# One layer of a gated trunk: who makes the low parts of the weights in the up stage

## The chip, the cores and the metric

The kernel runs on one core of a Trainium2 chip. The metric is the device time of one execution in microseconds (us). TensorE does the matrix products, VectorE (DVE in the rows), ScalarE (ACT) and GpSimd (POOL) do elementwise work, and SyncE (SP), ScalarE and GpSimd issue transfers between the memory (HBM) and the on-chip SBUF. Rows with a q (ACTq, SPq) are an engine's instructions that issue transfers. PSUM is where TensorE writes, in eight banks of 512 columns.

## What is computed

One layer with batch 1, 512 tokens and width 1024: windowed attention and retention, then the PEER mixer, which takes the experts from two tables of 16384 rows, then a gated embedding and norms. The part that matters here, cut:

```python
h = rms_norm(x, mix_norm);  z = h @ w_in          # attention and retention mixers, gates
x = x + merged @ w_out
# peer(h = rms_norm(x, ffn_norm)): 8 heads, each picks 16 of 128*128 experts per token
q = (h @ w_query).reshape(B, S, PEER_HEADS, 2, half)
s1, s2 = q[..., 0, :] . sk[0],  q[..., 1, :] . sk[1]
top_s, expert_idx = top 16 of v1 + v2;  gates = softmax(top_s)
u  = jnp.take(expert_down, idx, axis=0)
act = jax.nn.gelu(jnp.einsum('td,ted->te', hx, u))
vv = jnp.take(expert_up, idx, axis=0)
y  = jnp.einsum('te,ted->td', act * g, vv)
x = x + y
gate = sigmoid(rms_norm(x, ple_norm) @ w_ple_gate);  x = x + gate * (p @ w_ple_proj)
return rms_norm(x, final_norm)
```

The kernel computes `act` for all 16384 experts and all tokens but the last 128 as dense products, in 128 units of 128 experts, with the gates of the experts not chosen at zero; the last 128 tokens go over fetched rows.

## The kernel before

**Numbers in two parts.** A product in fp32 is made of three products in fp32r: each operand is split into a high part (ScalarE's copy to fp32r) and a low part, the operand less the high part. `mm3` (lines 931 to 934) adds high x high, high x low and low x high in one bank.

**Weights.** All weights go through one ring of eight slots of 128x1024 (512 KB each), unit after unit in the order of `UNITS`: projections, then 128 units `dn` (the down table), 128 units `up` (the up table), two `pp`, eight `pg`. `UP0` is the number of the first up unit. For each unit SyncE reads the slot `raw` (line 480) once TensorE is done with the unit eight back (`wait_used`), ScalarE makes `w_hi` (line 550, `upper`, signal `hi_done`), and GpSimd makes `w_lo` as `raw - w_hi` (line 493, `lower`, signal `lo_done`). `raw` and `w_lo` lie at the same address, so `w_lo` is written in place. ScalarE runs `LEAD` = 5 units ahead in the two stages with the expert tables.

**Down stage.** For each unit `dn`, TensorE multiplies with h for the first 352 tokens (`down`), ScalarE applies gelu (line 754) and stores the activations in HBM. Beside it the gates are spread and stored, and GpSimd fetches rows of the down table for the remaining tokens (line 517), which VectorE multiplies and sums (line 1335, `dot`).

**Up stage.** For unit e, VectorE (`weigh`) multiplies activations and gates, read back by ScalarE in groups of four units (`read_back`, lines 790 and 793), to `wgt` (line 1754); ScalarE copies it to `b_hi` (line 846, `weight_upper`, two units ahead); VectorE makes `b_lo` (line 1763, signal `wgt_split`). Between the two, from unit 8 on, VectorE adds a fetched row of the up table times its activation into PSUM (`axpy`, lines 1740 and 1743), 128 rows in all, 15 in 16 units on the average, mostly one to a unit. TensorE (`up`) waits for `lo_done` and `wgt_split` of the unit and runs 18 matmuls of 512 columns: three tiles of tokens, two banks each, `mm3`. Six banks collect all 128 units.

**GpSimd's queue.** GpSimd goes through the units in one written order: wait for `hi_done` of unit u, make `w_lo`, then issue the fetches that stand at u. The fetches of the up table (line 529) stand from u = `UP0` + 5 on (`FETCH_UP`), each waits for its slot among ten (`V_SLOTS`): the first needs the gates stored and the embeddings split (`p_split`), the seventh all dots, the eleventh and later the `axpy` ten before it.

**ScalarE's order in the up stage** (`up_turn`), for unit e: `w_hi` of unit e + 5, then `b_hi` of unit e + 2, and at the end of each group of four a read-back.

Of the kernel before, what the change touches and what calls it, by code (L numbers as in the profile page):

```python
# [7 lines left out]
F32 = mybir.dt.float32  # L8
F32R = mybir.dt.float32r
U32 = mybir.dt.uint32  # L10
ALU = mybir.AluOpType
# [7 lines left out]
PH, NKEY, TOPK = 8, 128, 16  # L19
# [16 lines left out]
RING = 8  # L36
# [35 lines left out]
DN0, UP0 = UNIT[("dn", 0)], UNIT[("up", 0)]  # L72
# [66 lines left out]
FIRST_Z = 7  # L139
EXP_AT, SELECT_AT = 4, 6  # L140
AHEAD = 2
FINAL_DVE = 6
RAW_Q = 4

# [51 lines left out]
def block_program(nc, xT_d, w_d, small_d, rope_r_d, decay_d, rope_a_d, mask_d, pT_d, down_d, up_d, out_d):  # L196
# [14 lines left out]
    with ExitStack() as ctx:  # L211
# [3 lines left out]
        def sem(name):  # L215
            return ctx.enter_context(nc.semaphore(name))
# [3 lines left out]
        w_hi = sb("w_hi", [P, RING, UW], F32R)  # L220
        with nc.sbuf_tensor("raw", [P, RING, UW], F32) as raw:
            pass
        w_lo = sb("w_lo", [P, RING, UW], F32R)
# [128 lines left out]
        landed = [sem(f"landed{i}") for i in range(RING)]  # L352
        hi_done = sem("hi_done")
        lo_done = sem("lo_done")
        proj_done = sem("proj_done")
        proj_free, pg_free = [sem("proj_free0"), sem("proj_free1")], sem("pg_free")
        tile_ready, tile_free = sem("tile_ready"), sem("tile_free")
# [132 lines left out]
        @block.gpsimd  # L490
        def _(pool):
            def lower(s):
                return nc.gpsimd.tensor_tensor(w_lo[:, s, :], raw[:, s, :], w_hi[:, s, :].bitcast(F32),  # L493
                                               ALU.subtract)

            first = min(FETCH_DOWN) // RING
            with pool.Fori(0, first) as r:
                for s in range(RING):
                    pool.wait_ge(hi_done, RING * r + (s + 1))
                    lower(s).then_inc(lo_done, 1)  # L500
            for u in range(first * RING, NU):
                pool.wait_ge(hi_done, u + 1)
                lower(u % RING).then_inc(lo_done, 1)
                for r in FETCH_DOWN.get(u, ()):
                    extra, n = row_of(r)
                    if r == 0:
                        pool.wait_ge(x_spilled, 16)
                        pool.wait_ge(sq_ready, 2 * KT)
                        pool.wait_ge(h_ready, 3 * KT)
                    if extra:  # L510
                        pool.wait_ge(extra_ready, 1)
                    elif n % TOPK == 0:
                        pool.wait_ge(expert_ready, n // TOPK + 1)
                    if r >= U_SLOTS:
                        pool.wait_ge(dot_done, r - U_SLOTS + 1)
                    ids = expert_extra if extra else expert_of
                    pool.indirect_dma_start(u_slot(r), None, down_d,
                                            bass.IndirectOffsetOnAxis(ap=ids[:, n:n + 1], axis=0)
                                            ).then_inc(u_landed[r % U_SLOTS], 16)
                for n in FETCH_UP.get(u, ()):  # L520
                    if n == 0:
                        for b in range(2):
                            pool.wait_ge(gate_written[b], 16 * (NTG // 2))
                        pool.wait_ge(p_split, 2)
                    if n == V_OWN:
                        pool.wait_ge(dot_done, NROWS)
                    if n >= V_SLOTS:
                        pool.wait_ge(axpy_done, n - V_SLOTS + 1)
                    pool.indirect_dma_start(v_slot(n), None, up_d,
                                            bass.IndirectOffsetOnAxis(ap=expert_of[:, n:n + 1], axis=0)  # L530
                                            ).then_inc(v_landed[n % V_SLOTS], 16)
            for k in range(FINAL_DVE, KT):
                pool.wait_ge(x_ready, KT + k + 1 + (k == KT - 1))
                nc.gpsimd.tensor_scalar(final[:, k, :], xT[:, k, :], gains[:, 3, k:k + 1], None, ALU.mult
                                        ).then_inc(pool_scaled, 1)
            pool.wait_ge(pool_scaled, KT - FINAL_DVE)
            pool.wait_ge(rows_spread, 1)
            for k in range(FINAL_DVE, KT):
                nc.gpsimd.tensor_tensor(final[:, k, :], final[:, k, :], rrms, ALU.mult).then_inc(final_pool, 1)
# [3 lines left out]
        def _(sc):  # L543
# [304 lines left out]
            def up_turn(i):  # L848
                last = i == NKEY // STEP - 1
                for c in range(STEP):  # L850
                    e = STEP * i + c
                    upper(UP0 + LEAD + e, (UP0 + LEAD + e) % RING)
                    if not last or c + AHEAD < STEP:
                        weight_upper(e + AHEAD, (c + AHEAD) % STEP)
# [74 lines left out]
        def _(pe):  # L929
# [16 lines left out]
            def columns(key, r_hi, r_lo, kt=KT, u=None, at=0, width=P, tiles=None, at_tile={}):  # L946


                u = UNIT[key] if u is None else u
                pe.wait_ge(lo_done, u + 1)  # L950
                bank_free(key)
                s = u % RING
                for k in range(kt):
                    if tiles is not None:
                        pe.wait_ge(tiles[0], tiles[1] + k + 1)
                    if k in at_tile:
                        at_tile[k]()
                    o = k * width + at
                    ins = mm3(proj_bank(key), w_hi[:, s, o:o + P], w_lo[:, s, o:o + P],
                              r_hi[:, k, :], r_lo[:, k, :], k == 0, k == kt - 1)  # L960
                ins.then_inc(proj_done, 1)
# [263 lines left out]

            def up(i, c):
                e = STEP * i + c
                pe.wait_ge(lo_done, e + (UP0 + 1))
                pe.wait_ge(wgt_split, e + 1)
                first = isinstance(i, int) and i == 0 and c == 0  # L1230
                last = isinstance(i, int) and i > 0 and c == STEP - 1
                s = (UP0 + c) % RING
                for t in range(TDT):
                    a = slice(P * t, P * t + P)
                    for n, b in enumerate(UP_BANKS[t]):
                        if first and b == 0:
                            pe.wait_ge(act_ready, NKEY)
                        ins = mm3(bank[:, b, :], b_hi[:, c % 4, a], b_lo[:, c % 4, a],
                                  w_hi[:, s, 512 * n:512 * n + 512], w_lo[:, s, 512 * n:512 * n + 512], first, last)
                    if last and t < TDT - 1:  # L1240
                        ins.then_inc(up_tile_done, 1)
                ins.then_inc(up_done, 1)
# [40 lines left out]
                if m == 1:  # L1283
                    spread(2)
            last = UNIT[("pg", KT - 1)]
            pe.wait_ge(lo_done, last + 1)
            for x in range(2):
                pe.wait_ge(pg_free, KT - 4 + x)
                for k in range(KT):
# [13 lines left out]
        def _(ve):  # L1303
# [17 lines left out]
            tt, ts, stt = nc.vector.tensor_tensor, nc.vector.tensor_scalar, nc.vector.scalar_tensor_tensor  # L1321
# [424 lines left out]
            def weigh(e):  # L1746
# [13 lines left out]
                for n in ADD_UP_AT.get(e, ()):  # L1760
# [2 lines left out]
                tt(b_lo[:, c % 4, 0:TD], wgt[:, c % 2, :], b_hi[:, c % 4, 0:TD].bitcast(F32),  # L1763
                   ALU.subtract).then_inc(wgt_split, 1)

            for e in range(NKEY):
                weigh(e)

            def evict(t, b, at):

# [129 lines left out]
```

## Time and profile before

| | us |
|---|---|
| median of 3 runs | 1982.0 |
| lowest and highest | 1981.55, 1982.93 |
| span of the profiled execution | 1979.5 |
| TensorE busy in it | 1956.9 |
| VectorE, GpSimd, ScalarE busy | 1365.3, 1234.5, 806.0 |

The span runs from the first to the last instruction of one profiled execution; the runs are timed without a profile and include what lies around the span. The up stage lies between 1381 and 1904 us of the span. Engines overlap, so a busy time says nothing of the end by itself: what counts is whether TensorE waits.

### The profile page before, as it was taken

To read this page: it belongs to the slowest core of one execution; us is meant where nothing else is said; L and a number is where in the kernel's file an instruction comes from. 1 tells how busy PE (TensorE), PEld (TensorE's weight loads), DVE (VectorE), ACT (ScalarE), POOL (GpSimd) and SP (SyncE) were. 2 spreads that over 40 slices of the span, in tenths; PEclk is the share of its full clock that TensorE was granted. 3 is DMA by queue.
4 is the path that set the end of the run, shared out by engine and by line. 5 is a ranking of instruction groups with operands and counts; after the bars stand their busy time and mean duration, and the time that the engine had idled before them with its cause. 6 is when DMAs were issued, how large, how long until landed. Compare 5 with 4: busy or idle time off the path is not lost.

```text
span 1979.5 us, 27319 instructions
## 1 busy us (share of the span) xinstructions
PE 1956.9 (99%) x10232; PEld 1724.9 (87%) x10232; DVE 1365.3 (69%) x2287; ACT 806.0 (41%) x1272; POOL 1234.5 (62%) x686
## 2 busy tenths in 40 slices
PE   7999999999999999999999999999999999999998
PEld 6888888888888888999999999999888888888887
DVE  6433333332831489999968888861998999999976
ACT  5222222232553343433346666654333333333352
POOL 5343434352234433899997767766998988888842
PEclk9999999999999999999999999999999999999999
DMA  5222222233223332899997999998999999999931
GB/s 198 86 90 86 91 85 85 87 116 112 80 75 96 96 128 78 333 333 350 366 360 270 386 377 359 372 389 273 363 372 347 377 357 354 375 364 361 358 108 43
DMA packets 171953, 471.93 MB, mean 238 GB/s; under 512 B 13776, under 2 KB 62928, under 8 KB 170064
## 3 DMA queue, kind: packets, MB, share of 16 engines
q1 hardware_dynamic: 58032, 209.04, 30.5%
q0 software_dynamic: 41472, 151.01, 20.5%
q10 hardware_dynamic: 72352, 110.64, 15.6%
q8 instruction: 54, 0.88, 0.2%
q14 instruction: 43, 0.35, 0.0%
HBM read 413.49 MB, written 54.53 MB: 236 GB/s over the span
## 4 chain that ended last, share of the span: by engine, by line
PE 96%; DVE 2%; ACT 1%; DMA 0%; issue 0%; POOL 0%; POOLq 0%; SPq 0%; DVEq 0%; ACTq 0%
PE bank L932 29%; PE bank L934 29%; PE bank L933 29%; PE bank L1185 4%; PE bank L1047 1%; PE bank L1130 1%; PE bank L1115 1%; PE bank L1091 0%; PE bank L1101 0%; DVE bank L1375 0%; DMA xT<-x_cols 0%; PE bank L1016 0%; PE bank L1138 0%; ACT b_hi L594 0%; DVE h_lo L1383 0%; DVE scr L1422 0%
## 5 line engine op out<-in xcount | busy, mean ns | idle before, releaser
L493 POOL TENSOR_TENSOR w_lo<-raw,w_hi 128x1024 fp32r<-128x1024 f32 x390 | 937.3, 2412 | 650.1 <-ACT w_hi L550 646.9
L932 PE MATMUL bank<-h_hi,w_hi 128*128 128x352 f32 (+2 forms) x1560 | 549.1, 352 | 0.0
L934 PE MATMUL bank<-h_hi,w_lo 128*128 128x352 f32 (+2 forms) x1560 | 538.1, 345 | 0.0
L933 PE MATMUL bank<-h_lo,w_hi 128*128 128x352 f32 (+2 forms) x1560 | 537.2, 344 | 0.0
L550 ACT ACTIVATE w_hi<-raw 128x1024 fp32r<-128x1024 f32 x390 | 407.6, 1054 | 309.8 <-DMA raw<-weights 254.0
L933 PEld LDWEIGHTS bank<-h_lo,w_hi 128*128 128x128 f32 x1560 | 294.7, 189 | 19.7
L934 PEld LDWEIGHTS bank<-h_hi,w_lo 128*128 128x128 f32 x1560 | 293.0, 188 | 20.7
L932 PEld LDWEIGHTS bank<-h_hi,w_hi 128*128 128x128 f32 x1560 | 293.8, 188 | 19.5
L1763 DVE TENSOR_TENSOR b_lo<-scr,b_hi 128x384 fp32r<-128x384 f32 x128 | 267.3, 2088 | 46.3 <-ACT b_hi L846 46.1
L932 PE MATMUL bank<-w_hi,b_hi 128*128 128x512 f32 x768 | 298.9, 389 | 0.0
L934 PE MATMUL bank<-w_hi,b_lo 128*128 128x512 f32 x768 | 298.8, 389 | 0.0
L933 PE MATMUL bank<-w_lo,b_hi 128*128 128x512 f32 x768 | 298.8, 389 | 0.0
L932 PEld LDWEIGHTS bank<-w_hi,b_hi 128*128 128x128 f32 x768 | 144.2, 188 | 30.2 <-DVE b_lo L1763 0.5
L933 PEld LDWEIGHTS bank<-w_lo,b_hi 128*128 128x128 f32 x768 | 144.2, 188 | 30.0
L934 PEld LDWEIGHTS bank<-w_hi,b_lo 128*128 128x128 f32 x768 | 144.2, 188 | 29.8
L754 ACT ACTIVATE scr<-bank 128x352 f32<-128x352 f32 x128 | 58.7, 458 | 150.0 <-PE bank L934 149.9
L932 PE MATMUL bank<-b_hi,w_hi 128*128 128x512 f32 x272 | 108.2, 398 | 10.6 <-DVE b_lo L1350 9.2
L846 ACT ACTIVATE b_hi<-scr 128x384 fp32r<-128x384 f32 x128 | 66.7, 521 | 122.9 <-DVE scr L1754 122.5
L932 PE MATMUL bank<-w_hi,h_hi 128*128 128x512 f32 (+1 forms) x288 | 109.7, 381 | 1.1 <-DVE h_lo L1383 1.1
L934 PE MATMUL bank<-w_hi,h_lo 128*128 128x512 f32 (+1 forms) x288 | 108.8, 378 | 0.0
L933 PE MATMUL bank<-w_lo,h_hi 128*128 128x512 f32 (+1 forms) x288 | 108.7, 378 | 0.0
L1335 DVE SCALAR_TENSOR_TENSOR more<-more,bank 128x1024 f32<-128x1024 f32 x80 | 96.9, 1211 | 15.8 <-DMA more<-peer_down,scr 9.1
(227 smaller groups left out, 2705.0 us busy)
## 6 DMA issues: line engine op xcount, KB each, us to landing
raw<-weights SPq DMA_DIRECT2D x390, 512.0 KB, 6.2
act_scratch<-scr ACTq DMA_DIRECT2D x64, 384.0 KB, 7.1
gate_scratch<-scr ACTq DMA_DIRECT2D x12, 2048.0 KB, 13.5
scr<-gate_scratch ACTq DMA_DIRECT2D x22, 768.0 KB, 9.6
scr<-act_scratch ACTq DMA_DIRECT2D x22, 768.0 KB, 14.8
xT<-gate_scratch ACTq DMA_DIRECT2D x10, 768.0 KB, 8.9
xT<-act_scratch ACTq DMA_DIRECT2D x10, 768.0 KB, 14.9
scr<-scr ACTq DMA_DIRECT2D x20, 128.0 KB, 3.9
```

What stands on the lines that cost most here:

```text
L493: return nc.gpsimd.tensor_tensor(w_lo[:, s, :], raw[:, s, :], w_hi[:, s, :].bitcast(F32), ALU.subtract)
L550: nc.scalar.activation(w_hi[:, u_mod, :], raw[:, u_mod, :], ACT.Copy).then_inc(hi_done, 1)
L754: nc.scalar.activation(act[:, c % 4, 0:TZ], bank[:, c % 2, 0:TZ], ACT.Gelu_apprx_tanh).then_inc(act_ready, 1)
L846: nc.scalar.activation(b_hi[:, c % 4, 0:TD], wgt[:, c % 2, :], ACT.Copy).then_inc(wgt_hi_ready, 1)
L932: nc.tensor.matmul(out, a_hi, c_hi, start=first, stop=False)
L933: nc.tensor.matmul(out, a_hi, c_lo, start=False, stop=False)
L934: return nc.tensor.matmul(out, a_lo, c_hi, start=False, stop=last)
L1047: ins = nc.tensor.matmul(bank[:, 2 + j, 0:S - P * j], r_k[:, c, P * j:P * j + P], r_q[:, c, P * j:S], start=c == 0, stop=c == 1)
L1115: ins = nc.tensor.matmul(bank[:, 7, P * t:P * t + P], a_v[:, t - 1 + b, P * kv:P * kv + P], a_pT[:, t, b, :], start=b == 0 or t == 0, stop ...
L1185: ins = nc.tensor.matmul(scattered(q)[:, x, :], onehot(q, x, 0).bitcast(F32), gated[q % 4][:, x, :], start=True, stop=True)
L1335: stt(out=row, in0=row, scalar=1.0, in1=h_tok, op0=ALU.mult, op1=ALU.mult, accum_out=to[:, n:n + 1]).then_inc(dot_done, 1)
L1763: tt(b_lo[:, c % 4, 0:TD], wgt[:, c % 2, :], b_hi[:, c % 4, 0:TD].bitcast(F32), ALU.subtract).then_inc(wgt_split, 1)
```

## The change

In the up stage GpSimd makes `w_lo` of the first two units only (`OWN_LOW` = 2). VectorE makes the other 126 (`VE_LOW`), by `lower_up(e + 2)` behind `weigh(e)`, under a signal of its own, `up_lo_done`. TensorE's waits are renumbered. GpSimd keeps its row fetches in their written order, and the `w_lo` of all units before and after.

```diff
--- before.py
+++ after.py
@@ -139,6 +139,8 @@
 FIRST_Z = 7
 EXP_AT, SELECT_AT = 4, 6
 AHEAD = 2
+OWN_LOW = 2
+VE_LOW = NKEY - OWN_LOW
 FINAL_DVE = 6
 RAW_Q = 4
 
@@ -352,6 +354,7 @@
         landed = [sem(f"landed{i}") for i in range(RING)]
         hi_done = sem("hi_done")
         lo_done = sem("lo_done")
+        up_lo_done = sem("up_lo_done")
         proj_done = sem("proj_done")
         proj_free, pg_free = [sem("proj_free0"), sem("proj_free1")], sem("pg_free")
         tile_ready, tile_free = sem("tile_ready"), sem("tile_free")
@@ -499,8 +502,9 @@
                     pool.wait_ge(hi_done, RING * r + (s + 1))
                     lower(s).then_inc(lo_done, 1)
             for u in range(first * RING, NU):
-                pool.wait_ge(hi_done, u + 1)
-                lower(u % RING).then_inc(lo_done, 1)
+                if not UP0 + OWN_LOW <= u < UP0 + NKEY:
+                    pool.wait_ge(hi_done, u + 1)
+                    lower(u % RING).then_inc(lo_done, 1)
                 for r in FETCH_DOWN.get(u, ()):
                     extra, n = row_of(r)
                     if r == 0:
@@ -947,7 +951,7 @@
 
 
                 u = UNIT[key] if u is None else u
-                pe.wait_ge(lo_done, u + 1)
+                pe.wait_ge(lo_done, u + 1 if u < UP0 else u + 1 - VE_LOW)
                 bank_free(key)
                 s = u % RING
                 for k in range(kt):
@@ -1225,7 +1229,10 @@
 
             def up(i, c):
                 e = STEP * i + c
-                pe.wait_ge(lo_done, e + (UP0 + 1))
+                if isinstance(i, int) and e < OWN_LOW:
+                    pe.wait_ge(lo_done, e + (UP0 + 1))
+                else:
+                    pe.wait_ge(up_lo_done, e - (OWN_LOW - 1))
                 pe.wait_ge(wgt_split, e + 1)
                 first = isinstance(i, int) and i == 0 and c == 0
                 last = isinstance(i, int) and i > 0 and c == STEP - 1
@@ -1283,7 +1290,7 @@
                 if m == 1:
                     spread(2)
             last = UNIT[("pg", KT - 1)]
-            pe.wait_ge(lo_done, last + 1)
+            pe.wait_ge(lo_done, last + 1 - VE_LOW)
             for x in range(2):
                 pe.wait_ge(pg_free, KT - 4 + x)
                 for k in range(KT):
@@ -1763,8 +1770,16 @@
                 tt(b_lo[:, c % 4, 0:TD], wgt[:, c % 2, :], b_hi[:, c % 4, 0:TD].bitcast(F32),
                    ALU.subtract).then_inc(wgt_split, 1)
 
+            def lower_up(e):
+
+                s = (UP0 + e) % RING
+                ve.wait_ge(hi_done, UP0 + e + 1)
+                tt(w_lo[:, s, :], raw[:, s, :], w_hi[:, s, :].bitcast(F32), ALU.subtract).then_inc(up_lo_done, 1)
+
             for e in range(NKEY):
                 weigh(e)
+                if e + OWN_LOW < NKEY:
+                    lower_up(e + OWN_LOW)
 
             def evict(t, b, at):
 
```

On **VectorE**, at the start of the up stage (`scr` is the place of the activations and gates and of `wgt`), before and then after:

```order
L1754 TENSOR_TENSOR scr<-scr 128x384 [waits acts_landed0,gate_landed0]
L1763 TENSOR_TENSOR b_lo<-scr,b_hi 128x384 [waits wgt_hi_ready]
L1754 TENSOR_TENSOR scr<-scr 128x384
L1763 TENSOR_TENSOR b_lo<-scr,b_hi 128x384 [waits wgt_hi_ready]
L1754 TENSOR_TENSOR scr<-scr 128x384 [waits wgt_split]
L1763 TENSOR_TENSOR b_lo<-scr,b_hi 128x384 [waits wgt_hi_ready]
```

```order
L1761 TENSOR_TENSOR scr<-scr 128x384 [waits acts_landed0,gate_landed0]
L1770 TENSOR_TENSOR b_lo<-scr,b_hi 128x384 [waits wgt_hi_ready]
L1777 TENSOR_TENSOR w_lo<-raw,w_hi 128x1024 [waits hi_done]
L1761 TENSOR_TENSOR scr<-scr 128x384
L1770 TENSOR_TENSOR b_lo<-scr,b_hi 128x384 [waits wgt_hi_ready]
L1777 TENSOR_TENSOR w_lo<-raw,w_hi 128x1024 [waits hi_done]
L1761 TENSOR_TENSOR scr<-scr 128x384 [waits wgt_split]
L1770 TENSOR_TENSOR b_lo<-scr,b_hi 128x384 [waits wgt_hi_ready]
L1777 TENSOR_TENSOR w_lo<-raw,w_hi 128x1024 [waits hi_done]
```

A `w_lo` of 1024 columns now stands between the `b_lo` of one unit and the product of the next.

On **GpSimd**, at the seam of the down and the up stage (the seventeen `w_lo` ahead of the first fetch are those of the last eleven down units and the first six up units; x17 means seventeen alike in a row), before and then after:

```order
L493 TENSOR_TENSOR w_lo<-raw,w_hi 128x1024 [waits hi_done] x17
L529 DMA scr<-peer_up,scr 128x1024 [waits p_split,gate_written1,gate_written0]
L529 DMA scr<-peer_up,scr 128x1024
L493 TENSOR_TENSOR w_lo<-raw,w_hi 128x1024 [waits hi_done]
L529 DMA scr<-peer_up,scr 128x1024
L493 TENSOR_TENSOR w_lo<-raw,w_hi 128x1024 [waits hi_done]
```

```order
L496 TENSOR_TENSOR w_lo<-raw,w_hi 128x1024 [waits hi_done] x13
L533 DMA scr<-peer_up,scr 128x1024 [waits p_split,gate_written1,gate_written0]
L533 DMA scr<-peer_up,scr 128x1024 x5
L533 DMA more<-peer_up,scr 128x1024 [waits dot_done]
L533 DMA more<-peer_up,scr 128x1024 x3
L533 DMA scr<-peer_up,scr 128x1024 [waits axpy_done] x6
```

The first ten fetches now follow each other behind the `w_lo` of the second up unit, with no wait for a weight between them; the eleventh is the first that waits for a row addition (`axpy_done`).

## Rows read from the trace of the kernel before

**Rows 1.** The page: busy us of each engine (share of the span), instructions.

```profile
PE 1956.9 (99%) x10232; PEld 1724.9 (87%) x10232; DVE 1365.3 (69%) x2287; ACT 806.0 (41%) x1272; POOL 1234.5 (62%) x686
```

**Rows 2.** Windows: length, busy us of PE, PEld, DVE, ACT, POOL, clock, DMA share, GB/s.

```profile
1340.00:1381.00 41.00, 41.00 (x258) 41.00 (x257) 4.80 (x7) 17.68 (x25) 26.29 (x11) 1.00 0.85 272
...
1512.00:1643.00 131.00, 130.97 (x579) 108.14 (x578) 123.74 (x99) 48.83 (x65) 115.86 (x68) 1.00 1.01 366
...
1773.00:1904.00 131.00, 131.00 (x580) 108.51 (x579) 117.58 (x96) 49.16 (x65) 106.44 (x59) 1.00 0.90 324
```

**Rows 3.** TensorE in order of time: start us, us, engine, line, output<-inputs.

```profile
1381.49 0.39 PE L932 MATMUL bank<-w_hi,b_hi 128*128 128x512 f32 x1
...
1505.29 0.39 PE L932 MATMUL bank<-w_hi,b_hi 128*128 128x512 f32 x1
1505.51 0.39 PE L933 MATMUL bank<-w_lo,b_hi 128*128 128x512 f32 x1
...
1903.87 1.25 PEld L1255 LDWEIGHTS bank<-small,scr 128*128 128x128 f32 x10
```

**Rows 4.** The waits of TensorE in the stage, then what stands behind the one.

```profile
PEld bank L932 <- DVE b_lo L1763: 0.5, 1, 0.5
...
1510.14 6.25 ACTq L793 DMA_DIRECT2D scr<-act_scratch  x1
...
1517.94 2.45 DVE L1763 TENSOR_TENSOR b_lo<-scr,b_hi 128x384 fp32r<-128x384 f32 x1 [2.18 <-ACT b_hi L846]
```

**Rows 5.** Groups of the stage: busy us, mean ns | idle before, releaser.

```profile
L493 POOL TENSOR_TENSOR w_lo<-raw,w_hi 128x1024 fp32r<-128x1024 f32 x129 | 311.3, 2415 | 52.1 <-ACT w_hi L550 50.2
...
L1763 DVE TENSOR_TENSOR b_lo<-scr,b_hi 128x384 fp32r<-128x384 f32 x127 | 266.8, 2100 | 34.3 <-ACT b_hi L846 34.2
```

**Rows 6.** GpSimd and VectorE side by side, in order of time.

```profile
1500.45 2.39 POOL L493 TENSOR_TENSOR w_lo<-raw,w_hi 128x1024 fp32r<-128x1024 f32 x1
...
1501.19 2.08 DVE L1763 TENSOR_TENSOR b_lo<-scr,b_hi 128x384 fp32r<-128x384 f32 x1
...
1503.00 1.10 POOL L529 DMA_INDIRECT scr<-peer_up,scr  x1 [0.16 <-issue]
...
1503.19 0.55 DVE L1754 TENSOR_TENSOR scr<-xT 128x384 f32<-128x384 f32 x1
```

**Rows 7.** VectorE in order of time, where the feeders catch up.

```profile
1701.91 0.55 DVE L1754 TENSOR_TENSOR scr<-xT 128x384 f32<-128x384 f32 x1
1702.38 1.27 DVE L1743 SCALAR_TENSOR_TENSOR bank<-more,scr,bank 128x1024 f32<-128x1024 f32 x1
1703.57 2.09 DVE L1763 TENSOR_TENSOR b_lo<-scr,b_hi 128x384 fp32r<-128x384 f32 x1
1705.58 0.55 DVE L1754 TENSOR_TENSOR scr<-xT 128x384 f32<-128x384 f32 x1
```

**Rows 8.** The seam of down and up stage, GpSimd, ScalarE and VectorE, by time.

```profile
1370.48 4.77 POOL L493 TENSOR_TENSOR w_lo<-raw,w_hi 128x1024 fp32r<-128x1024 f32 x2 [4.10 <-ACT w_hi L550]
...
1374.91 1.06 ACT L550 ACTIVATE w_hi<-raw 128x1024 fp32r<-128x1024 f32 x1 [0.43 <-ACT scr L754]
...
1378.77 0.56 DVE L1763 TENSOR_TENSOR b_lo<-scr,b_hi 128x384 fp32r<-128x384 f32 x1 [11.96 <-ACT b_hi L846]
...
1381.70 0.46 ACT L754 ACTIVATE scr<-bank 128x352 f32<-128x352 f32 x1 [0.39 <-PE bank L934]
...
1383.13 1.46 ACTq L793 DMA_DIRECT2D xT<-act_scratch  x1
...
1386.14 2.45 DVE L1763 TENSOR_TENSOR b_lo<-scr,b_hi 128x384 fp32r<-128x384 f32 x1 [4.73 <-ACT b_hi L846]
...
1388.32 1.09 POOL L529 DMA_INDIRECT scr<-peer_up,scr  x1
```

**Rows 9.** Groups of VectorE by form, over the whole span.

```profile
L1690 DVE TENSOR_TENSOR b_lo<-bank,scr 128x1024 fp32r<-128x1024 f32 x48 | 58.7, 1222 | 14.4 <-PE bank L1185 14.3
```

**Rows 10.** The weight reads of line 480 issued in the up stage.

```profile
DMA to landing us min/median/max: 3.3/7.2/10.1
```


## The prediction

> **What bounds the kernel now.** I read the page first, then the windows of the up stage, then TensorE's rows at its two ends, then what VectorE and GpSimd do in one unit of it. The page gives TensorE 1956.9 us of the 1979.5 us span [rows 1]. The windows of the up stage, four of 130 to 131 us from 1381 to 1904 us of which the second and the fourth stand in the rows, show TensorE busy in all but 0.03 us, at the full granted clock, with the DMA engines marked busy nearly all the time and 324 to 366 GB/s moved [rows 2]. So in the stage that the change touches nothing but TensorE's own stream sets the pace.
>
> That stream can be measured at its ends. The first up matmul starts at 1381.49 us, and the transposes behind the last one are loaded at 1903.87 us [rows 3]: 522.38 us for 128 units of 18 matmuls, 226.7 ns each, **4.08 us a unit**. Two rows in the middle have the same step, 1505.29 to 1505.51 [rows 3]. TensorE waits once in the whole stage, 0.5 us, for a low part of the weighted activations [rows 4]. That is all that a change of the feeders can give back here.
>
> Who feeds it: per unit GpSimd makes w_lo, 2415 ns in the mean [rows 5], and issues a row fetch, 1.10 us [rows 6]. VectorE multiplies activations and gates (L1754), adds a fetched row (L1743) and makes b_lo (L1763). Where the feeders catch up, VectorE starts a unit at 1701.91 and the next at 1705.58 us [rows 7], a step of 3.67 us, just over the 2.41 + 1.10 of GpSimd, so it runs at GpSimd's pace. Two rows show why: b_lo takes 0.56 us at 1378.77 [rows 8] but 2100 ns in the mean [rows 5]. The one at 1501.19 us ends at 1503.27, 0.43 us after the end (1502.84) of the w_lo that GpSimd started at 1500.45 [rows 6]. The two operations exclude each other. This costs slack and no time, as 3.67 is below 4.08.
>
> **What is taken away.** 126 of the 129 w_lo of the stage leave GpSimd, 304 of their 311.3 us [rows 5]. With them the exclusion goes: b_lo, 266.8 us now [rows 5], should take 0.56 us each, some 71 us. On the path to the end this is worth the one wait, **-0.5 us**. Its history: ScalarE was held for 6.25 us, from 1510.14, in issuing a read of activations; b_hi was so late that b_lo started only at 1517.94, took 2.45 us, and ended at 1520.39 us [rows 4]. With 0.56 in place of 2.45 it would have been ready 1.9 us earlier, more than the 0.5 that were missing. I take the whole 0.5.
>
> **What is added.** 126 operations of 128x1024 on VectorE with two sources in SBUF. None of that size and those sources stands in the trace. Bounds: not under the one of 384 columns, 0.56 us [rows 8], and not over GpSimd's own 2.41 us for the same tile [rows 5]. The nearest row is VectorE's 1024-column operation with one source in PSUM, 1222 ns [rows 9], and I take that. An operation starts some 0.08 us before the one ahead has ended: L1754 to L1743 is 0.47 us, L1743 to L1763 is 1.19 [rows 7]. VectorE's unit is then 0.47 + 1.19 + 0.48 + 1.14 = 3.28 us, and 3.36 with the second row addition of every fifteenth unit. TensorE's is 4.08, so **VectorE stays faster by 0.72 us a unit** (now by 0.41), and the added work costs nothing. TensorE's stream hides it; that cover is gone only if w_lo takes more than 1.14 + 0.72 = 1.86 us up to the next start. By the Trainium skill ("VectorE: DVE Perf Modes", the part on mode 2x_2P) an fp32 tensor_tensor stays at one element a cycle, since both read ports are taken; 0.96 GHz makes an estimate of 1.07 us plus a fixed part, and the sum would not change.
>
> **The waits that are added.** lower_up(e+2) stands behind b_lo(e) and waits for w_hi of unit e+2. ScalarE makes that one a turn before b_hi(e), for which b_lo(e) has just waited, so in the loop the wait is always met. At the seam w_hi(3) starts at 1374.91 us and w_hi(2) before it, both ahead of VectorE's first b_lo at 1378.77 [rows 8]: met too. TensorE's wait for w_lo is met two units ahead, and b_lo stays what comes last. Queued behind the new operation is the product of the next unit, and behind that b_hi and b_lo. At the seam w_lo(2) delays the second product by 1.14 us, and with it ScalarE. There the last down activation, at 1381.70, had waited 0.39 us for TensorE [rows 8], so it moves by 0.75 and ends at 1382.9; TensorE wants it (for the bank of its third tile) 12 matmuls after 1381.49, at 1384.2. The read issue of 1383.13 moves to 1383.9 and lasts 1.46, and b_lo(2) starts 1.55 us after it as now [rows 8] and ends at 1387.5 us, for a unit due at 1381.49 + 2 x 4.08 = 1389.65. Now it ends at 1386.14 + 2.45 = 1388.59 [rows 8], the thinnest margin of the seam. Cost: nothing.
>
> **What moves without being written.** In GpSimd's queue the fetches for unit u stood behind the w_lo of unit u and so behind its w_hi. Now nothing paces them but free slots. The ten slots are free when GpSimd leaves w_lo(1), the first of the two that start at 1370.48 [rows 8], at about 1372.9 us. So ten fetches of 512 KB go out by about 1385, where now the first leaves at 1388.32 us [rows 8]. The stretch that they move into carries 272 GB/s [rows 2], and after it the queue is quiet until the first row addition. In the loop a fetch then leaves when a slot comes free, one each 4.3 us as now, and the bytes are the same in all. Beside the burst weights must still land: those of unit u are asked for when unit u-8 is done, and have 4 units less 2.4 us (w_hi, b_hi, b_lo and hand-offs), **13.9 us**, until b_lo(u-3) is late. Now they land in 7.2 us in the stage's median and 10.1 at most [rows 10]. Cost taken: nothing; its bounds are the first rival.
>
> The up loop on TensorE also loses seven register instructions; its rows have no gap where they stand, so nothing comes of it. The pp and pg weights stay on GpSimd, and what follows 1904 us is untouched.
>
> **Sum**: 0 (added) - 0.5 (the wait) + 0 (burst) = -0.5 us on the span of 1979.5. The three runs have a median of 1982.0, 2.5 us over the span, and I carry that over: **1981.5 us**. A measurement of this kernel can tell about 0.2%, 4 us, so this is "no change".
>
> **Rivals.**
>
> *The burst holds the weights (slower).* If the weight reads had to queue behind the ten fetches, 5.24 MB at 366 GB/s [rows 2] are 14.3 us, and a weight tile would land after 7.2 + 14.3 = 21.5 us, 7.6 over the allowed 13.9, once: **1989 us**. It decides from a landing time of 13.9 us. A milder form goes by ScalarE: the read issue at 1383.9 held for 6.25 us as at 1510.14 [rows 4] puts the end of b_lo(2) at 1392.2, 2.6 us late: 1984. For: the DMA engines are marked full in the stage [rows 2]. Against: weights land in 7.2 us now with a fetch in flight nearly always. Chance 6% for over 4 us, and 8% for the mild form, which counts as same.
>
> *Fetch issues hold VectorE (slower).* If the issue of a fetch excluded VectorE's two-source operations as w_lo does, its 1.10 us [rows 6] would come on top of VectorE's 3.36: 4.46 us a unit, 0.38 over TensorE's, times 120 units, +46 us: **2027 us**. It decides from 0.72 us held per unit. The trace speaks against it: the product at 1503.19 takes 0.55 us inside the fetch of 1503.00 to 1504.10, and the b_lo of 1501.19 ends 0.27 us into that fetch [rows 6]. Chance 2%. The Trainium skill ("SBUF — State Buffer", on the shared port pair) says that a VectorE operation with two SBUF inputs and a GpSimd operation that reads SBUF exclude each other for the whole instruction, and a fetch takes its row numbers from SBUF; these two rows don't bear that out for it.
>
> *VectorE is as slow at w_lo as GpSimd (slower).* At 2.41 us its unit is 3.36 - 1.14 + 2.33 = 4.55 us, 0.47 over, times 126: +59 us, **2040 us**. The row of 1222 ns is against it. Chance 1%.
>
> *The change doesn't do what it says*: should b_lo stay long or the wait come back elsewhere, the time is **1982**, within same. *TensorE is freed (faster)*: for over 4 us of gain its step of 226.7 ns would have to shrink by 1.7 ns, but the mean over the stage, in which w_lo alone keeps GpSimd busy for 311 us [rows 5], equals the step at 1505.29 [rows 3], when the fetch of 1503.00 has ended and no w_lo runs. Chance 2%.
>
> **How the numbers follow.** The forecast with its near forms (up to 3 us lost, or the wait kept) has 89%, of it 8% for the mild loss; burst 6%, ports 2%, slow w_lo 1%, faster 2%. So same 0.89, slower 0.09, faster 0.02. The range takes the runs' own spread (1981.55 to 1982.93) about 1981.5, the mild loss above and a microsecond below: 1980.3 to 1984.8.
>
> **What the profile after would show.** Right: TensorE's up stage 522 us long and without a wait; w_lo on VectorE near 1.22 us; b_lo near 0.56 us throughout; ScalarE waiting less for VectorE and more for weights; GpSimd's busy time down by some 300 us and VectorE's by 266.8 - 71 - 154 = 42; ten fetches from 1373 to 1385 us; weight landings under 13.9 us. Wrong: waits of TensorE for b_lo in units 2 to 8 (burst), w_lo or b_lo lengthened beside fetches (ports), or a VectorE that never rests in the stage (slow w_lo).

## The result, and the profile after

| | before | after |
|---|---|---|
| median of the runs, us | 1982.4 (4 runs) | 1992.1 (4 runs) |
| lowest and highest, us | 1981.55, 1982.93 | 1990.08, 1992.70 |
| span of the profiled execution, us | 1979.5 | 1990.9 |

The ratio is 1.005, with a 95% interval of 1.0037 to 1.0062: slower by some 10 us, where no change was forecast.

The page of the changed kernel, engines as in [rows 1]:

```profile
PE 1957.9 (98%) x10232; PEld 1724.6 (87%) x10232; DVE 1308.0 (66%) x2413; ACT 803.7 (40%) x1272; POOL 975.7 (49%) x560
```

GpSimd has lost 259 us and VectorE 57, as the edit meant. TensorE is busy 1 us longer, and the span is 11.4 us longer: TensorE waits somewhere. The windows of the up stage, columns as in [rows 2], say where:

```profile
1381.00:1512.00 131.00, 122.38 (x532) 100.61 (x531) 96.37 (x120) 47.44 (x64) 43.45 (x30) 0.97 0.95 344
1512.00:1643.00 131.00, 131.00 (x580) 108.47 (x579) 108.90 (x131) 48.29 (x64) 49.12 (x35) 1.00 0.99 363
1643.00:1773.00 130.00, 130.00 (x575) 107.67 (x574) 108.67 (x130) 47.74 (x64) 44.76 (x34) 1.00 0.99 362
1773.00:1904.00 131.00, 131.00 (x580) 108.47 (x579) 108.71 (x126) 47.12 (x63) 45.35 (x27) 1.00 0.90 326
```

The last three windows are full. All of the loss lies in the first, and all of TensorE's waits of the stage are these two (the waits, from 1384 us on: us in total, times, longest):

```profile
PE bank L936 <- DVE b_lo L1770: 7.3, 1, 7.3
PE bank L936 <- issue: 1.3, 1, 1.3
```

The first and the last of the ten fetches, then ScalarE, VectorE and TensorE, each in order of time; this is the seam of [rows 8]:

```profile
1373.28 0.95 POOL L533 DMA_INDIRECT scr<-peer_up,scr  x1
...
1386.85 0.94 POOL L533 DMA_INDIRECT more<-peer_up,scr  x1 [1.14 <-issue]
...
1385.61 0.46 ACT L758 ACTIVATE scr<-bank 128x352 f32<-128x352 f32 x1 [2.77 <-remote]
1386.53 0.43 ACTq L794 DMA_DIRECT2D xT<-gate_scratch  x1
1387.05 9.88 ACTq L797 DMA_DIRECT2D xT<-act_scratch  x1
1396.98 1.06 ACT L554 ACTIVATE w_hi<-raw 128x1024 fp32r<-128x1024 f32 x1 [10.16 <-issue]
1397.94 0.51 ACT L850 ACTIVATE b_hi<-scr 128x384 fp32r<-128x384 f32 x1
...
1398.48 0.56 DVE L1770 TENSOR_TENSOR b_lo<-scr,b_hi 128x384 fp32r<-128x384 f32 x1 [14.40 <-ACT b_hi L850]
...
1386.12 0.50 PE L936 MATMUL bank<-w_hi,b_hi 128*128 128x512 f32 x1 [1.32 <-issue]
...
1391.49 0.39 PE L938 MATMUL bank<-w_hi,b_lo 128*128 128x512 f32 x1
1399.18 0.77 PE L936 MATMUL bank<-w_hi,b_hi 128*128 128x512 f32 x1 [7.30 <-DVE b_lo L1770]
1399.75 0.63 PE L937 MATMUL bank<-w_lo,b_hi 128*128 128x512 f32 x1
1400.18 0.63 PE L938 MATMUL bank<-w_hi,b_lo 128*128 128x512 f32 x1
...
1403.59 0.40 PE L937 MATMUL bank<-w_lo,b_hi 128*128 128x512 f32 x1
```

Read it upwards. TensorE stops behind unit 1 and goes on at 1399.18, when b_lo(2) has ended (1398.48 + 0.56). b_lo(2) waited for b_hi(2), started at 1397.94. ScalarE came to it late because the instruction ahead, the issue of the third read-back's activations, lasted 9.88 us, where the same row took 1.46 in [rows 8]. While it lasted, the data of the ten fetches were still being moved. The share of the 16 DMA engines' time by queue while the issue was held, 1387 to 1397 us of the changed kernel (packets, MB, share):

```profile
q0 software_dynamic: 608, 2.22, 55.2%
q1 hardware_dynamic: 364, 1.36, 34.1%
q10 hardware_dynamic: 345, 0.50, 13.4%
```

q0 is GpSimd's queue, q1 SyncE's (the weights), q10 ScalarE's. ScalarE's queue moved 0.50 MB in these 10 us. In the kernel before, in the ten microseconds from the same issue (1383 to 1393 us), it moves 1.97 MB in 58.1% of the engines' time, and q0 only 0.45 MB.

**Where the 11.4 us go.** TensorE's next matmul was due at 1391.72 (0.23 us a step) and came at 1399.18: 7.46. The ten matmuls from there start 0.43 to 0.57 us apart and take 4.41 us where ten take 2.27: 2.14; the granted clock is 0.50 from 1399.1 to 1403.5 us, the lower level (1.2 GHz), after TensorE had stood for 7.5 us. The wait of 1.3 us lies at 1386.12, ahead of TensorE's thirteenth up matmul, 1.47 with its step. The first up matmul starts at 1381.89, 0.40 later than in [rows 3]. The old wait of 0.5 [rows 4] is gone. 7.46 + 2.14 + 1.47 + 0.40 - 0.50 = 11.0 of 11.4 us.

In the 1.3 us wait TensorE stands for ScalarE's last down activation, which ends at 1386.07; ScalarE had stood for 2.77 us ahead of it, though the last down matmul had started at 1381.73. Of the profiled executions this one alone has it: not a second profile of the same kernel (below), nor the three other kernels with the same burst. It stays unexplained, and how often it comes is open: two of the three runs without a profile took 1992.0 and 1992.3 us, as long as this one (1992.7). The later start of the first matmul is no loss of the change: it is there before anything changed, in GpSimd's `w_lo` at 1364.39 against 1363.99 us, and over the kernels below this start lies anywhere between 1380.95 and 1382.55.

### The profile page after: what moved, and what is told of

Read it like the earlier page. It is cut to its first block, busy times and chain, and to the rows that moved or that the text cites. A ratio compares the mean times of both kernels' runs of the same rounds, so it can differ in the third digit from the quotient of the medians.

```text
span 1990.9 us, 27221 instructions
## 1 busy us (share of the span) xinstructions
PE 1957.9 (98%) x10232; PEld 1724.6 (87%) x10232; DVE 1308.0 (66%) x2413; ACT 803.7 (40%) x1272; POOL 975.7 (49%) x560
## 4 chain that ended last, share of the span: by engine, by line
PE 93%; DVE 3%; ACT 1%; issue 1%; ACTq 1%; DMA 0%; another core or an unknown queue 0%; POOL 0%; POOLq 0%; SPq 0%; DVEq 0%
PE bank L936 28%; PE bank L938 28%; PE bank L937 28%; PE bank L1189 4%; PE bank L1051 1%; PE bank L1134 1%; PE bank L1119 1%; ACTq L797 0%; PE bank L1095 0%; PE bank L1105 0%; DMA xT<-x_cols 0%; DVE bank L1382 0%; DVE scr L1682 0%; ACT w_hi L554 0%; PE bank L1020 0%
## 5 line engine op out<-in xcount | busy, mean ns | idle before, releaser
L496 POOL TENSOR_TENSOR w_lo<-raw,w_hi 128x1024 fp32r<-128x1024 f32 x264 | 635.8, 2421 | 630.2 <-ACT w_hi L554 627.5
L533 POOL DMA_INDIRECT scr<-peer_up,scr x78 | 108.9, 1396 | 204.6 <-DVE bank L1750 174.5
L1777 DVE TENSOR_TENSOR w_lo<-raw,w_hi 128x1024 fp32r<-128x1024 f32 x126 | 153.8, 1220 | 0.0
L1770 DVE TENSOR_TENSOR b_lo<-scr,b_hi 128x384 fp32r<-128x384 f32 x128 | 72.2, 564 | 111.5 <-ACT b_hi L850 110.7
L533 POOL DMA_INDIRECT more<-peer_up,scr x50 | 72.8, 1456 | 106.8 <-DVE bank L1750 104.7
```

The source lines that it names most:

```text
L533: pool.indirect_dma_start(v_slot(n), None, up_d, bass.IndirectOffsetOnAxis(ap=expert_of[:, n:n + 1], axis=0)).then_inc(v_landed[n % V_SLOT ...
L1777: tt(w_lo[:, s, :], raw[:, s, :], w_hi[:, s, :].bitcast(F32), ALU.subtract).then_inc(up_lo_done, 1)
```

## The experiments

The theory now: **the burst of ten fetches crowds out ScalarE's queue, its issue instruction is held, and b_hi(2), b_lo(2) and TensorE follow**. The rivals: the new w_lo on VectorE delays the seam, or the weights land late. Each ratio below is to runs of the kernel before that were taken with the experiment (medians 1981.8 to 1982.6 us).

### The old pace back, VectorE keeps w_lo

In GpSimd's loop of the changed kernel the wait of every unit comes back; the subtraction does not:

```diff
 for u in range(first * RING, NU):
+    pool.wait_ge(hi_done, u + 1)
     if not UP0 + OWN_LOW <= u < UP0 + NKEY:
-        pool.wait_ge(hi_done, u + 1)
         lower(u % RING).then_inc(lo_done, 1)
```

> The changed kernel with one wait put back: in GpSimd's queue each up unit again waits for its w_hi before the fetches that stand at it; VectorE still makes w_lo. Theory A (the ten fetches that go out at once at the seam hold ScalarE's issue of the third read-back, and so TensorE): the read issue at the seam is back under 3 us, TensorE waits under 1 us in the up stage, 1982.4 us within 1.5, 9 to 10 below the changed kernel. Theory B (VectorE's w_lo at the seam delays the chain product, b_hi, b_lo): nothing changes against the changed kernel, 1990 to 1992 us.

Measured: 1981.4 us (10 runs), 0.9996 of before (0.9987 to 1.0006), span 1979.6. TensorE has no wait in the stage. The issue, in order of time:

```profile
1384.15 2.25 ACTq L797 DMA_DIRECT2D xT<-act_scratch  x1
```

All w_lo of the changed kernel are still on VectorE, so neither their time nor their place at the seam is the loss. One wait in GpSimd's queue is: it had kept the fetches apart.

Two later issues are long in this kernel as well, 6.38 us at 1411.04 and 4.53 us at 1541.03, with no burst beside them, and TensorE doesn't wait: behind the first of them b_lo(10) starts at 1418.98, for a unit due at 1381.88 + 10 x 4.08 = 1422.7. So a held issue costs by where it stands. At the seam the next unit's b_lo has far less room.

### The burst alone, GpSimd keeps w_lo

The kernel before, with the first ten fetches moved up to where the change lets them go:

```diff
-    FETCH_UP.setdefault(UP0 + LEAD + up_unit_of(_n), []).append(_n)
+    FETCH_UP.setdefault(UP0 + (1 if _n < V_SLOTS else LEAD + up_unit_of(_n)), []).append(_n)
```

> The kernel before with one thing changed: its first ten fetches of the up stage stand behind the w_lo of the second up unit, so that they go out at 1373 to 1386 us as in the changed kernel. GpSimd makes all w_lo. Theory A: the read issue at the seam is held 5 to 10 us again, TensorE waits 4 to 8 us, 1988 to 1992 us. Theory B: no loss of more than 1.5 us against 1982.4, as VectorE has no w_lo. A part of the loss could be GpSimd's own w_lo of units 2 and 3, which start only at 1387 us and are due at 1389.7 and 1393.7; then TensorE waits for w_lo and not for b_lo.

Measured: 1994.4 us (4 runs), 1.0061 (1.0044 to 1.0078), a little over what was expected. ScalarE, then GpSimd and VectorE, then TensorE:

```profile
1383.04 10.16 ACTq L793 DMA_DIRECT2D xT<-act_scratch  x1
...
1388.59 11.56 POOL L493 TENSOR_TENSOR w_lo<-raw,w_hi 128x1024 fp32r<-128x1024 f32 x5
...
1394.75 5.82 DVE L1763 TENSOR_TENSOR b_lo<-scr,b_hi 128x384 fp32r<-128x384 f32 x1 [13.43 <-ACT b_hi L846]
...
1400.71 0.77 PE L932 MATMUL bank<-w_hi,b_hi 128*128 128x512 f32 x1 [10.96 <-DVE b_lo L1763]
```

The burst alone, with no w_lo on VectorE, holds the issue for 10.16 us, 0.3 more than in the changed kernel. The wait is longer, 10.96 in place of 7.30 us, since here the exclusion of [rows 6] works too: GpSimd makes five w_lo in a row, and b_lo takes 5.82 us beside them instead of 0.56.

### The same burst, the read-back two turns later

The changed kernel, with the third read-back issued behind b_hi of unit 3 and not ahead of the loop:

```diff
                     if not last or c + AHEAD < STEP:
                         weight_upper(e + AHEAD, (c + AHEAD) % STEP)
+                    if e == 1:
+                        read_back(2)
...
-            read_back(2)
             for i in range(NKEY // STEP - 1):
                 up_turn(i)
```

> The changed kernel, in which ScalarE issues the third read-back (gates and activations of units 8 to 11) two units later, behind b_hi of unit 3. The ten fetches go out as in the changed kernel. Theory A, first form (the hold of ScalarE in its issue is the link): b_hi(2) and b_hi(3) are on time and TensorE's wait at unit 2 is gone; the issue may still be held, but with 3 or 4 us left of it, and the time is 1983 to 1986 us. Second form (the weights of units 5 to 8 land too late behind the fetches): TensorE's wait stays at 5 us or more, 1988 us or over. Theory B: 1990 to 1992 us.

Measured: 1981.5 us (10 runs), 1.0001 (0.9991 to 1.0010), better than expected. The fetches stand as before, 1372.85 to 1386.03 us, and GpSimd's queue takes 58.0% of the DMA engines' time from 1380 to 1390. The issues are held all the same, two of them now:

```profile
1387.51 6.74 ACTq L797 DMA_DIRECT2D xT<-act_scratch  x1
...
1398.50 5.26 ACTq L797 DMA_DIRECT2D scr<-act_scratch  x1
```

But b_lo(2) starts at 1384.83 and b_lo(3) at 1387.59, and behind the first held issue b_lo(4) starts at 1395.80, for a unit due 4 x 4.08 us behind the first matmul, at 1397.8. TensorE has no wait. A late weight would have cost the same here; so it is the place of the held instruction on ScalarE that costs, and not the weights.

### The same number of fetches, an eighth of the bytes

The changed kernel; the first ten fetches bring 128 columns in place of a row's 1024, 512 bytes each, and VectorE reads these eight times over. The kernel leaves out the rest of these rows, and with them a part of the result for the last 128 tokens:

```diff
+                    short = n < V_SLOTS
-                    pool.indirect_dma_start(v_slot(n), None, up_d,
+                    pool.indirect_dma_start(v_slot(n)[:, 0:P] if short else v_slot(n), None,
+                                            up_d.rearrange("e (a n) -> (e a) n", n=P) if short else up_d,
```

> The changed kernel, in which each of the first ten fetches brings 512 B a row in place of 4 KB (wrong rows, spread over the 1024 columns; the output of the last 128 tokens is wrong, VectorE does the same number of columns). As many instructions and rows at the same time, an eighth of the bytes, 0.66 MB in place of 5.24. Theory A by bytes (the engines are taken up by the fetches' data): the read issue at the seam is under 3 us and the time 1982 to 1984 us. By count (issues or rows): the hold stays at 5 us or more, 1988 us or over.

Measured: 1982.1 us (10 runs), 1.0002 (0.9992 to 1.0011). The ten fetches are issued at 1373.97 to 1386.65 us, as closely as in the changed kernel. The issue, and the queues from 1380 to 1390 us:

```profile
1384.81 2.10 ACTq L799 DMA_DIRECT2D xT<-act_scratch  x1
...
q10 hardware_dynamic: 1647, 1.26, 41.9%
q1 hardware_dynamic: 288, 1.05, 33.5%
q0 software_dynamic: 207, 0.41, 14.1%
```

It is the bytes of the burst that hold ScalarE, not the number of fetches or GpSimd's issuing.

### Six free, the rest paced

The changed kernel, with the old wait for four of the ten (`elif UP0 + LEAD + 5 <= u < UP0 + LEAD + V_SLOTS + 1: pool.wait_ge(hi_done, u + 1)`):

> The changed kernel, in which only the first six fetches of the up stage go out unpaced; the seventh to the eleventh wait again for w_hi of the unit at which they stand. Dose of theory A: four fetches of 0.52 MB fewer ahead of the read issue, at about 0.4 MB a us some 5 us less of backlog, so a hold of 3 to 6 us in place of 9.9, a wait of TensorE of 0 to 3 us, and 1982 to 1985 us, between the paced kernel (1981.4) and the changed one (1992.1). Were the number of fetches without weight, for instance if any unpaced fetch at this place does it, 1990 us or over.

Measured: 1988.7 us (6 runs), 1.0031 (1.0019 to 1.0044). This expectation missed. ScalarE's issues and TensorE in the rows:

```profile
1383.21 6.71 ACTq L799 DMA_DIRECT2D xT<-act_scratch  x1
...
1392.17 0.66 PE L938 MATMUL bank<-w_hi,b_hi 128*128 128x512 f32 x1 [2.87 <-DVE b_lo L1772]
...
1395.62 0.43 PE L940 MATMUL bank<-w_hi,b_lo 128*128 128x512 f32 x1
...
1448.22 10.81 ACTq L799 DMA_DIRECT2D scr<-act_scratch  x1
...
1461.18 0.50 PE L938 MATMUL bank<-w_hi,b_hi 128*128 128x512 f32 x1 [1.87 <-DVE b_lo L1772]
...
1484.21 9.18 ACTq L799 DMA_DIRECT2D xT<-act_scratch  x1
...
1495.56 0.50 PE L938 MATMUL bank<-w_hi,b_hi 128*128 128x512 f32 x1 [1.45 <-DVE b_lo L1772]
```

Six fetches, 3.1 MB, still hold the issue for 6.71 us. Behind the wait of 2.87 us (3.0 without a matmul) eight matmuls take 3.45 us (1392.17 to 1395.62) where 1.81 is usual, so a wait of this size has a clock cost too, 1.6 us. And where the pacing ended, GpSimd issued eight fetches within 12 us (1424.42 to 1436.23): a second burst, and behind it issues held for 10.81 and 9.18 us, each with a wait of TensorE. That the second burst holds both is not shown by a run of its own. 2.87 + 1.64 + 1.87 + 1.45 = 7.8 us; from its first up matmul to the first matmul behind the stage this kernel takes 530.9 us (1380.95 to 1911.86) and the kernel before 522.6, so nearly all of the stage's loss is in them. The rest of the 9.1 us that the span (1988.6) is over before lies outside the stage.

### Activations first, gates behind

Each read-back issues first the gates and then the activations. The changed kernel, with these two the other way round in the third read-back only:

> The changed kernel with the two reads of the third read-back in the other order: activations (256 pieces of 3 KB) first, gates (1536 pieces of 512 B) second. If ScalarE is held because the pieces of the first read still fill what its queue can take, the many pieces of the gates do it: the activations' issue is now short, the gates' issue, second, is held less or not at all (under 6 us), and the time falls below 1988 us. If ScalarE is held by whatever comes second, or for as long as the fetches take up the engines, the second issue lasts about 10 us as before and the time stays at 1990 to 1993 us.

Measured: 1984.8 us (10 runs), 1.0015 (1.0006 to 1.0025). The issues in order of time:

```profile
1382.91 0.40 ACTq L798 DMA_DIRECT2D xT<-act_scratch  x1
1383.33 0.53 ACTq L800 DMA_DIRECT2D xT<-gate_scratch  x1
...
1393.33 5.59 ACTq L795 DMA_DIRECT2D scr<-gate_scratch  x1
1399.01 6.69 ACTq L798 DMA_DIRECT2D scr<-act_scratch  x1
```

At the seam nothing is held, in the middle of the same burst (56.3% for GpSimd's queue). The next read-back is, for 5.59 + 6.69 us, and TensorE waits 2.2 us at 1407.95. The profiled execution is the fastest of the ten (1983.0 us); where the others, up to 1987.7, lose more is not in this trace. The rows fit a queue of ScalarE's with room for so much and no more, which an issue has to wait for: the gates' many small pieces fill it, and what comes next is held. That is a reading and not shown, nor is how the room would be counted.

### The changed kernel once more

> The changed kernel once more, unaltered, for a second profile. Theory A: the read issue at the seam is held 8 to 11 us again, TensorE waits for b_lo(2) 5 to 8 us, and the clock falls for some 4 us behind that wait; 1990 to 1993 us. Open is whether the 1.3 us wait of TensorE for the last down activation (its release came 3.5 us late in the first profile) comes again: if it belongs to the mechanism it does, if not TensorE has no wait before unit 2.

Measured: 1990.0 us (5 runs), 1.0040 (1.0026 to 1.0054), span 1987.8. ScalarE, TensorE, and windows with the clock (columns as in [rows 2]):

```profile
1384.39 9.90 ACTq L797 DMA_DIRECT2D xT<-act_scratch  x1
...
1390.05 0.39 PE L938 MATMUL bank<-w_hi,b_lo 128*128 128x512 f32 x1
1396.55 0.77 PE L936 MATMUL bank<-w_hi,b_hi 128*128 128x512 f32 x1 [6.11 <-DVE b_lo L1770]
...
1396.00:1401.00 5.00, 4.45 (x12) 3.59 (x13) 4.17 (x6) 2.43 (x4) 0.00 (x0) 0.59 1.08 364
1401.00:1406.00 5.00, 5.00 (x24) 4.14 (x23) 4.06 (x6) 2.85 (x4) 0.00 (x0) 1.00 0.75 261
```

The same hold to 0.02 us, again a wait for b_lo(2), and no other wait. 6.27 (1396.55 - 1390.28) + 1.73 (eight matmuls in 3.54 us in place of 1.81) + 0.60 (first up matmul at 1382.09) - 0.5 = 8.1 of the 8.3 us over before.

### How near VectorE is to its limit

The paced kernel of the first experiment, in which from unit 10 on VectorE makes one more subtraction of the w_lo kind per unit, whose result nothing uses: 512 columns in the first kernel, 1024 in the second (there with 0:2 and 2:4 in place of 0:1 and 2:3).

```diff
+                if e >= 10:
+                    tt(h_lo[:, 0:1, :], h_hi[:, 0:1, :].bitcast(F32), h_hi[:, 2:3, :].bitcast(F32),
+                       ALU.subtract)
```

> The paced kernel (GpSimd's fetches wait for w_hi again) with an operation more in each VectorE unit from unit 10 on: 512 columns, two sources in SBUF, its result unused. It measures the margin that the prediction gave VectorE, 0.72 us a unit. The operation lasts 0.69 us and takes 0.61 up to the next start: VectorE's unit becomes 3.36 + 0.61 = 3.97 us, under TensorE's 4.08. If the sum of the prediction was right: no loss, 1981.4 us within 1.5, TensorE waits under 1 us. If VectorE's unit really is near TensorE's already (more than 0.2 us missing in my sum): 120 x 0.1 to 0.4 us, 1990 us or over.

> As the run with half an operation more, but with 1024 columns, 1.22 us and 1.14 up to the next start: VectorE's unit becomes 4.50 us, 0.42 over TensorE's, for 116 units. What slack VectorE has ahead (3 to 5 us) is used up first. By the sum of the prediction: 2025 to 2035 us, TensorE waiting for b_lo in most units, VectorE never idle. If VectorE has more room than I give it: under 2015 us.

Measured: 1981.3 us (10 runs), 0.9997 (0.9987 to 1.0006), and 2029.7 us (4 runs), 1.0241 (1.0224 to 1.0258). The windows from 1500 to 1600 us of the one and of the other:

```profile
1500.00:1600.00 100.00, 100.00 (x443) 82.80 (x442) 97.68 (x125) 37.09 (x49) 34.85 (x27) 1.00 1.01 366
```

```profile
1500.00:1600.00 100.00, 98.39 (x404) 73.75 (x404) 99.90 (x114) 33.38 (x45) 74.35 (x24) 1.00 0.91 322
```

And one unit of VectorE in the second:

```profile
1600.79 0.55 DVE L1761 TENSOR_TENSOR scr<-scr 128x384 f32<-128x384 f32 x1
...
1602.92 1.21 DVE L1778 TENSOR_TENSOR h_lo<-h_hi 128x1024 fp32r<-128x1024 f32 x1
1604.05 1.21 DVE L1780 TENSOR_TENSOR w_lo<-raw,w_hi 128x1024 fp32r<-128x1024 f32 x1
1605.19 0.55 DVE L1761 TENSOR_TENSOR scr<-scr 128x384 f32<-128x384 f32 x1
```

VectorE's unit is 4.40 us with 1.13 to 1.14 us more in it, so 3.27 without, where the prediction worked out 3.28, and TensorE's is 4.08. Half an operation more fits, a whole one doesn't. By the margin of 0.72 us a whole one should cost 1.14 - 0.72 = 0.42 us in each of 116 units, 48.7 us; it costs 48.3 over the paced kernel.

## Why the prediction was wrong, point by point

**Right: what is added.** w_lo on VectorE takes 1220 ns in the mean over 126, where 1222 was taken from the nearest row [rows 9]; b_lo 564 ns over the stage, where 0.56 was taken; the groups of the stage (busy us, mean ns | idle before, releaser):

```profile
L1777 DVE TENSOR_TENSOR w_lo<-raw,w_hi 128x1024 fp32r<-128x1024 f32 x126 | 153.8, 1220 | 0.0
...
L533 POOL DMA_INDIRECT scr<-peer_up,scr x73 | 104.2, 1427 | 203.2 <-DVE bank L1750 174.5 <-DVE bank L1747 28.4 <-issue 0.3
...
L1770 DVE TENSOR_TENSOR b_lo<-scr,b_hi 128x384 fp32r<-128x384 f32 x127 | 71.6, 564 | 99.5 <-ACT b_hi L850 98.7
```

The margin of 0.72 us a unit holds (last experiment). w_lo has no idle time before it, so the waits that it adds on VectorE are always met, as said. TensorE has no wait after the seam, and the one of [rows 4] is gone. The changed kernel doesn't show that the shorter b_lo is the reason, as none of its issues after the seam lasts over 2.5 us; the paced kernel speaks for it, with an issue of 6.38 us and no wait. The stage still goes at TensorE's pace: with the burst tamed the changed kernel measures what the one before does, 1981.4.

**Right: the burst's place.** Ten fetches "by about 1385" from 1372.9 were forecast, and they stand at 1373.28 to 1386.85. Weights do land in under 13.9 us: 9.1 at most in the second profile.

**Wrong: the price of the burst, "Cost taken: nothing".** The step that failed is the sentence that put its condition on the landing of weights, 13.9 us. Weights were never the link: in the second profile of the changed kernel those issued in the up stage land in 6.9 us in the median, and moving ScalarE's read-back alone, with the burst kept, took the whole loss away. What the burst reached was an instruction of a compute engine, the issue of a read on ScalarE. The sum for the seam had carried it at its old length ("lasts 1.46"), with nothing for the burst beside it; it lasted 9.88 and 9.90 us.

**The mechanism stood in a rival, under-priced.** The mild form of "the burst holds the weights" had exactly this chain, from the read issue at 1383.9. It was priced with the longest hold of the trace of before, 6.25 us [rows 4], seen beside one fetch at a time; the ten together hold it 9.9 us, in both profiles. By the prediction's own arithmetic (1.55 us from the issue's end to b_lo, 0.56 for b_lo) 9.9 puts the end of b_lo(2) at 1383.9 + 9.9 + 1.55 + 0.56 = 1395.9, 6.3 us late for 1389.65, and not 2.6. That sum holds in the rows: 1384.39 + 9.90 + 1.55 + 0.56 = 1396.40, and TensorE goes on at 1396.55. From an issue at 1384.39 and a unit due at 1390.28 the hold that costs nothing is 3.8 us; the paced kernel (2.25) and the one with short rows (2.10) lie under it, the one with six fetches free (6.71) over it.

**Wrong: a wait counted at its length.** No term stood for the clock. Behind a wait of 6 to 7 us the traces show eight to ten matmuls at the lower level, 1.7 to 2.1 us more. With both corrections the forecast would have been 1981.5 + 6.3 + 1.9 = 1989.7, against 1992.1 and 1990.0 measured. The profile of the first holds 1.5 us of a wait that has no cause yet and 1.2 us that follow from it: the same late activation puts the read issue 2.66 us later than in the second profile (1387.05 against 1384.39), and the unit is due only 1.44 later.

**Wrong: the chance.** 14% went to all forms of this rival, on the ground that weights land in 7.2 us with a fetch in flight nearly always. One fetch in flight says little of ten: DMA shares of queues, which the argument did not look at, change from 0% to 75 and 58% for GpSimd's from 1380 to 1390 us, in the two profiles of the changed kernel.

**Fallen: the other rivals.** Fetch issues don't hold VectorE: in the kernels of the last experiment w_lo, b_lo and the product keep 1.21, 0.55 and 0.55 us while GpSimd issues. VectorE's w_lo is 1.22 and not 2.41 us. GpSimd's busy time fell by 259 and not 300 us, since each fetch issue lasts 1.43 us in the mean instead of 1.09; nothing waited for it. VectorE's fell by 57 and not 42: the two groups give 41, and an estimate for most of the rest is that operations overlap by 0.08 to 0.09 us, which busy time counts once, and each of 126 w_lo adds one such overlap, some 11 us.

## What to carry to other kernels

A wait that stands in an in-order queue also paces the transfers behind it; who takes it away with its work should look where the next free transfers go and put the pace back if it is a stretch with no slack. Price a burst not only at the landing of the data that the bottleneck needs, but at every instruction that issues a transfer on a compute engine, and at what stands behind that instruction. And a stop of TensorE costs more than its length where the granted clock falls: count the slow matmuls behind it.

None of the versions beats the kernel before: the paced one and the one with the late read-back lie at 0.9996 and 1.0001 of it, because TensorE's own stream, 522 us in the stage, sets the time whoever makes w_lo.

## What the runs showed of the hardware

- The instruction with which ScalarE issues a read of 768 KB took 9.88, 9.90 and 10.16 us beside ten fetches from another engine's queue, 6.71 us beside six, and 2.10 us beside ten of an eighth of the bytes. For that time ScalarE does nothing else. Without a burst it is mostly short but not always: 6.25 us in the kernel before [rows 4], 6.38 in the paced one.
- The queues don't share evenly. While the issue at the seam was held behind the burst (five profiles), GpSimd's took 55 to 60% of the DMA engines' time, SyncE's 28 to 34%, and ScalarE's, which has the smallest pieces, 13 to 17%. The Trainium skill ("DMA: Bandwidth & Descriptors", Queues, rings and completion order) has each DMA engine go round the queues packet by packet, a packet being several descriptors. The rows can't test that: their packets are single pieces (q0 counts some 1440 for the 1280 rows of the ten fetches), so how many of them make a turn isn't shown.
- A fetch issue of GpSimd lasted 0.95 us beside an idle VectorE, 1.43 in the mean beside a VectorE that also makes w_lo, and the two-source operations of VectorE did not lengthen. With w_lo on GpSimd it is VectorE's operation that lengthens, up to 5.82 us beside five w_lo in a row.
- After TensorE had stood for 3.0, 6.3, 7.5 and 11.1 us, the granted clock was at its lower level for the next 3.5, 3.5, 4.4 and 4.4 us; after 1.6 to 2.3 us the next matmuls took their usual 0.23 us a step but for the first.
